# Exclusive-or search end, context steps in VectorE's two waits, and ten more gathered steps ahead of the build

## The reference

```python
q = (xb @ w_query).reshape(t, PEER_HEADS, 2, HALF_KEY)
s = jnp.einsum('thik,hink->thin', q, sub_keys)
v_half, i_half = lax.top_k(s, TOPK)                      # best 16 of 128, for each half
cand = v_half[:, :, 0, :, None] + v_half[:, :, 1, None, :]
cand_idx = i_half[:, :, 0, :, None] * N_KEYS + i_half[:, :, 1, None, :]
top_v, top_pos = lax.top_k(cand, TOPK)                   # best 16 of the 256 sums
idx = take_along_axis(cand_idx, top_pos)                 # expert numbers
g = softmax(top_v)
act = gelu(einsum('thkd,td->thk', expert_u[idx], xb))
out = einsum('thk,thkd->td', g * act, expert_v[idx])
```

## Time and profile before

| what | value |
|---|---|
| median of 3 runs | 2578.82 us (2571.86 to 2583.09) |
| the profiled execution: its own time | 2583.05 us |
| its span, first to last instruction | 2581.2 us |
| TensorE busy | 2300.2 us (89%) |
| VectorE busy | 1797.7 us (70%) |
| POOL busy / ScalarE busy | 1179.9 us (46%) / 635.8 us (25%) |
| DMA: moved, mean | 705.28 MB, 273 GB/s |

### The profile page before, as it was taken

One profiled execution on the slowest core, in us unless ns is written; L12 is line 12 of the kernel. 1 busy time (PEld: TensorE's weight loads), 2 busy tenths in 40 slices (PEclk: granted clock), 3 DMA queues, 4 the chain that ended last, 5 costly groups with the idle time before them and its releaser, 6 DMA issues.

```text
span 2581.2 us, 26507 instructions
## 1 busy us (share of the span) xinstructions
PE 2300.2 (89%) x8779; PEld 1451.1 (56%) x8779; DVE 1797.7 (70%) x3184; ACT 635.8 (25%) x1564; POOL 1179.9 (46%) x979
## 2 busy tenths in 40 slices
PE   6988888898899997999989999978799999999960
PEld 1545454454566443487668887856566666644420
DVE  2657676645600789778778898899676767657678
ACT  2325435231211113411322112199111111110010
POOL 0022231221000346667542235477557786876865
PEclk8999999999999998999999999999899999999985
DMA  8211101107585678999874578999999999999997
GB/s 308 74 33 58 41 24 41 49 33 296 164 284 178 213 298 324 370 369 413 320 268 160 223 280 322 351 365 412 417 379 419 378 411 409 383 400 372 414 389 288
DMA packets 235577, 705.28 MB, mean 273 GB/s; under 512 B 22910, under 2 KB 47614, under 8 KB 234052
## 3 DMA queue, kind: packets, MB, share of 16 engines
q0 software_dynamic: 117936, 429.44, 43.1%
q1 hardware_dynamic: 116948, 272.27, 28.4%
q10 hardware_dynamic: 576, 2.10, 0.2%
HBM read 690.23 MB, written 13.50 MB: 273 GB/s over the span
## 4 chain that ended last, share of the span: by engine, by line
PE 31%; DVE 22%; POOL 17%; DMA 15%; issue 11%; ACT 3%; SPq 1%; DVEq 0%; ACTq 0%; POOLq 0%
PE bank L960 13%; POOL arena L1785 7%; POOL arena L1777 7%; DMA arena<-in_peer_v,arena 6%; DMA arena<-in_peer_u,arena 6%; PE bank L809 4%; PE bank L854 2%; DVE arena L2205 2%; DVE arena L2183 2%; DVE arena L1966 2%; PE bank L1112 2%; POOL arena L1834 2%; DVE arena L2129 2%; DVE arena L2126 2%; DVE arena L2128 1%
## 5 line engine op out<-in xcount | busy, mean ns | idle before, releaser
L1777 POOL DMA_INDIRECT arena<-in_peer_u,arena x384 | 489.1, 1274 | 577.7 <-DVE arena L2183 326.5
L2205 DVE SCALAR_TENSOR_TENSOR arena<-arena 128x1024 f32<-128x1024 f32 x381 | 495.3, 1300 | 139.0 <-DMA arena<-in_peer_v,arena 134.3
L2183 DVE CUSTOM_DVE_ANT_0 arena<-arena 128x1024 f32<-128x1024 f32 x384 | 476.4, 1247 | 150.2 <-DMA arena<-in_peer_u,arena 149.6
L1785 POOL DMA_INDIRECT arena<-in_peer_v,arena x384 | 463.9, 1208 | 244.0 <-DVE arena L2205 136.8
L960 PE MATMUL bank<-arena 128*128 128x512 f32 (+1 forms) x1472 | 507.2, 507 | 15.3 <-DMA arena<-in_w_in 5.2
L1220 PE MATMUL bank<-arena 128*128 128x512 f32 x1024 | 452.3, 594 | 13.4 <-DVE arena L2381 9.3
L1182 PE MATMUL bank<-arena 128*128 128x256 f32 x2048 | 455.3, 380 | 7.1 <-ACT arena L1634 6.4
L1182 PEld LDWEIGHTS bank<-arena 128*128 128x128 f32 x2048 | 390.6, 191 | 88.4 <-issue 37.4
L960 PEld LDWEIGHTS bank<-arena 128*128 128x128 f32 x1472 | 282.4, 193 | 236.0 <-issue 201.1
L1220 PEld LDWEIGHTS bank<-arena 128*128 128x128 f32 x1024 | 195.0, 191 | 232.7 <-issue 214.4
L1634 ACT ACTIVATE arena<-bank 128x256 f32<-128x256 f32 x128 | 49.0, 383 | 589.4 <-PE bank L1182 589.4
(11 more groups left out here) (260 smaller groups left out, 2476.6 us busy)
## 6 DMA issues: line engine op xcount, KB each, us to landing
arena<-in_peer_ut SPq DMA_DIRECT2D x128, 512.0 KB, 6.5
arena<-in_peer_v SPq DMA_DIRECT2D x128, 512.0 KB, 6.6
arena<-in_w_in SPq DMA_DIRECT2D x22, 2048.0 KB, 8.1
arena<-in_w_ada_t POOLq DMA_DIRECT2D x32, 512.0 KB, 4.0
arena<-in_w_ssd_out SPq DMA_DIRECT2D x8, 2048.0 KB, 13.2
arena<-in_w_query SPq DMA_DIRECT2D x8, 2048.0 KB, 7.9
arena<-in_w_ada SPq DMA_DIRECT2D x4, 2048.0 KB, 16.3
arena<-in_w_fourier SPq DMA_DIRECT2D x4, 2048.0 KB, 7.7
```

What stands on the lines that cost most here:

```text
L1777: nc.gpsimd.indirect_dma_start(rowbuf[slot], None, a["peer_u"], bass.IndirectOffsetOnAxis(ap=entries(IDX, k), axis=0)).then_inc(row_in[slo ...
L1785: nc.gpsimd.indirect_dma_start(rowbuf[slot], None, a["peer_v"], bass.IndirectOffsetOnAxis(ap=entries(IDX, k), axis=0)).then_inc(row_in[slo ...
L2183: V.tensor_tensor_reduce(out=rowbuf[slot], in0=rowbuf[slot], in1=h2c if item < PH else h2a[:, item // PH - 1, :], scale=1.0, scalar=0.0, o ...
L2205: STT(pv, rowbuf[slot], w, pv, ALU.mult, ALU.add).then_inc(s("vc_used"), 1)
```

## The change

It has three parts. The index lookup of `top` is written in 16-bit integers: each index gets 128 x its place added, the found place is multiplied by 128 too and written twice side by side, the two are combined by an exclusive-or, and the minimum over the sixteen is the index. The table `WITH` gets an entry `POS` of five context steps, which VectorE takes ahead of its wait for x and `pos1`, with a place for gates on ScalarE ahead of the row copies; 12 context steps stand ahead of the search and 11 in it. The gathered steps of tiles 1 and 2 are spread over heads 2 to 7 (32 as before), and `APART_EARLY` goes from 24 to 34, so that 66 and not 56 stand ahead of the build.

```diff
+        "GB1": (3, 3, 3, 3), "SO2": (2, 2, 2, 2), "SO3": (2, 2, 2, 2), "POS": (5, 0, 0, 0),
...
-CTX_BESIDE = (5, 5, 5, 5, 0, 0, 0, 0)
-APART_BESIDE = (0, 0, 0, 0, 8, 8, 8, 8)
-APART_TOP_BESIDE = {2: (0, 1), 6: (2, 3)}
-APART_EARLY = 24
+AHEAD_OF_SEARCH = 12
+CTX_BESIDE = (5, 5, 1, 0, 0, 0, 0, 0)
+APART_BESIDE = (0, 0, 4, 4, 6, 6, 6, 6)
+APART_TOP_BESIDE = {1: (0, 1), 5: (2, 3)}
+APART_EARLY = 34
...
-NORM_TOPS = PH + min(pair[0] for j, pair in APART_TOP_AT.items() if j > NORM_STEP)
+NORM_TOPS = PH + min((pair[0] for j, pair in APART_TOP_AT.items() if j > NORM_STEP), default=2 * PH)
...
             take_so("l", "SO3")                                  # ScalarE
+            between("l", "POS", 0)
             take_rows(8, (0, 1, 2, 3), 1)
...
+            between("l", "POS", 1)
             for n, t in enumerate(WO_ORDER):
...
-            row16 = shp[:, 6, 0:TOPK].unsqueeze(1).broadcast_to([P, 2, TOPK])
-            CP(places[:, 2:4, :], row16)
-            TS(places[:, 0:2, :], row16, float(TOPK), None, ALU.mult)
+            TS(key_place, shp[:, 6, 0:TOPK], float(NKEY), None, ALU.mult)
+            V.memset(shifts[:, 0:1], float(NKEY // TOPK))
+            V.memset(shifts[:, 1:2], float(NKEY))
...
-                CP(i16fs[:, 0:2 * n * TOPK], i16s[:, 0:2 * n * TOPK])
+                TT(flat(i16fs), flat(i16s), key_place.unsqueeze(1).broadcast_to([P, 2 * n, TOPK]), ALU.add)
...
-                ch(TT(e4, place.unsqueeze(2).broadcast_to([P, 2 * n, TOPK, TOPK]),
-                      flat(tijs).unsqueeze(3).broadcast_to([P, 2 * n, TOPK, TOPK]), ALU.is_equal))
-                ch(TT(e4, e4, flat(i16fs).unsqueeze(2).broadcast_to([P, 2 * n, TOPK, TOPK]), ALU.mult))
+                twice = tij16s[:, 0:4 * n * TOPK].rearrange("p (h q c) -> p h q c", h=2, c=2)
+                ch(TT(twice, tijs[:, 0:2 * n * TOPK].rearrange("p (h q) -> p h q", h=2).unsqueeze(3).broadcast_to([P, 2, n * TOPK, 2]),
+                      shifts.unsqueeze(2).unsqueeze(3).broadcast_to([P, 2, n * TOPK, 2]), ALU.mult))
+                e4 = cands[:, 0:256 * n].bitcast(U16).rearrange("p (g k m) -> p g k m", g=2 * n, m=TOPK)
+                by_two = [P, 2 * n, TOPK, TOPK // 2, 2]
+                ch(TT(e4.rearrange("p g k (m c) -> p g k m c", c=2),
+                      flat(i16fs).rearrange("p g (m c) -> p g m c", c=2).unsqueeze(2).broadcast_to(by_two),
+                      tij16s[:, 0:4 * n * TOPK].rearrange("p (g k c) -> p g k c", g=2 * n, c=2).unsqueeze(3).broadcast_to(by_two),
+                      ALU.bitwise_xor))
...
-                    ch(V.tensor_reduce(flat(picks), e4, AX.X, ALU.add))
+                    ch(V.tensor_reduce(flat(picks), e4, AX.X, ALU.min))
...
             merge("l", "SO3")                                    # VectorE
+            beside("l", "POS", 0)
             dve.wait_ge(s("x1_in"), 16)
...
-            context_steps(8)
+            context_steps(AHEAD_OF_SEARCH)
```

More of the change, by code:

```diff
@@ L15 @@
 U32 = mybir.dt.uint32
+U16 = mybir.dt.uint16
 I32 = mybir.dt.int32
@@ L130 @@
         "Z2": (2, 2, 2, 2), "Z3": (2, 2, 2, 2), "GB0": (3, 3, 3, 3), "SO0": (2, 2, 2, 2), "SO1": (2, 2, 2, 2),
-        "GB1": (3, 3, 3, 3), "SO2": (2, 2, 2, 2), "SO3": (2, 2, 2, 2), "WO0": (1, 1, 1, 1), "WO1": (1, 1, 1, 1)}
[2 rows of a table added]
 TOPS_AT = {2: (2, 3), 14: (4, 5), 26: (6, 7)}
@@ L356, in layer_kernel @@
         stat = sb("stat", [P, 64])
-        places = sb("places", [P, 4, TOPK], U32)
+        places = sb("places", [P, 2, TOPK], U32)
+        key_place, shifts = places[:, 0, :], places[:, 1, 0:2].bitcast(F32)
         masks = sb("masks", [P, 2, TOPK], U32)
@@ L472, in layer_kernel @@
         ij_w = [at(kb, 2 * PICKS).rearrange("p (t n) -> p t n", t=2) for kb in (139.25, 140.25)]
-        ij_all = at(139.25, 4 * PICKS).rearrange("p (g n) -> p g n", g=4)
+        ij_all = at(139.25, 2 * PICKS).bitcast(BF16).rearrange("p (g n) -> p g n", g=4)
         d_w = at(109, 2 * PICKS).rearrange("p (t n) -> p t n", t=2)
@@ L499, in layer_kernel @@
         four = at(122, 4 * 64).rearrange("p (i n) -> p i n", i=4)
-        v16s, i16s, tijs, picks = four[:, 0], four[:, 1].bitcast(U32), four[:, 2].bitcast(U32), four[:, 3]
+        v16s, i16s, tijs, picks = four[:, 0], four[:, 1].bitcast(U32), four[:, 2].bitcast(U32), four[:, 3].bitcast(BF16)
         small64 = at(124, 64)
         tvs, tps = small64[:, 0:32], small64[:, 32:64].bitcast(U32)
-        i16fs = small[:, 2].bitcast(BF16)
+        i16fs = small[:, 2].bitcast(U16)
+        tij16s = small[:, 3:5].rearrange("p a b -> p (a b)").bitcast(U16)
         dots = [small[:, 7, 0:TOPK], small[:, 11, 0:TOPK]]
@@ L2164, in top @@
                       ALU.bitwise_and))
-                e4 = cands[:, 0:256 * n].bitcast(BF16).rearrange("p (g k m) -> p g k m", g=2 * n, m=TOPK)
-                place = places[:, 0:4:3 - n, :]
-                ch(TT(e4, place.unsqueeze(2).broadcast_to([P, 2 * n, TOPK, TOPK]),
-                      flat(tijs).unsqueeze(3).broadcast_to([P, 2 * n, TOPK, TOPK]), ALU.is_equal))
-                ch(TT(e4, e4, flat(i16fs).unsqueeze(2).broadcast_to([P, 2 * n, TOPK, TOPK]), ALU.mult))
+                twice = tij16s[:, 0:4 * n * TOPK].rearrange("p (h q c) -> p h q c", h=2, c=2)
[7 more added lines that the diff above has]
+                      ALU.bitwise_xor))
                 if t in WHOLE:
-                    V.tensor_reduce(ij_all[:, :, TOPK * h:TOPK * h + TOPK], e4, AX.X, ALU.add).then_inc(s("topw_done"), n)
+                    V.tensor_reduce(ij_all[:, :, TOPK * h:TOPK * h + TOPK], e4, AX.X, ALU.min).then_inc(s("topw_done"), n)
                 else:
-                    ch(V.tensor_reduce(flat(picks), e4, AX.X, ALU.add))
+                    ch(V.tensor_reduce(flat(picks), e4, AX.X, ALU.min))
                     half = picks[:, 0:n * TOPK], picks[:, n * TOPK:2 * n * TOPK]
```

## The result

The kernel got slower: 2611.42 us (2603.11 to 2616.6, four runs) against 2580.36 (2571.86 to 2583.09) for the kernel before, a ratio of 1.0122 (1.0101 to 1.0144). The forecast was 2582 us and a range of 2561 to 2598, so it lies outside. The medians are 31.1 us apart, so 11 of these are not in the two traces.

A forecast was written before the change was run, and what follows sets the result against it. VectorE's finish of the build and the gathered rows then left set the end. Terms +15.1 + 17.8 - 24.8 - 2.3 - 1.8 + 25.4 - 26.3 = +3.1 us gave 2586.2, or 2582 against the median; own range 2573 to 2592, widened to 2561 to 2598.

The forecast's parts named there:

- The search end: VectorE's double tops: each saves 0.91 us with the exclusive-or at 692 ns; twelve ahead of the build, 10.9 us.
- Rival C: VectorE's tops: the exclusive-or runs at 1.225 us, +6.4 us, 2588 us; counted within the forecast's class, no chance of its own.
- The first wait: ScalarE's gates(6), ahead of the row copies, wait for the 112th u product and move TensorE's chain by 15.1 us.
- The second wait: VectorE ahead of the search waits at `weights(7)` for ScalarE's gates(7) until 1372.2; this adds 17.8 us.
- Rival A: Ahead of the search: the new waits don't bite, as product and gates come early enough; -25 us, 2554 us; chance 0.27.
- The ten steps: Ten more gathered steps on VectorE before the build cost 25.4 us, bounds 25 and 30.
- The rows given back: After the build: twenty fewer gathered rows are left, 10.5 MB at 399 GB/s, saving 26.3 us; bounds 12.8 and 31.
- Rival B: Tail: rows are not given back, only ten v additions leave it; +16.6 us, 2595 us; chance 0.23 with other path lengthening.
- is ahead of VectorE: Before the build: TensorE no longer stands 6.4 us for the search, its blocks end about 8 us later, ahead of VectorE.

The follow-up runs named there:

- e6: The kernel before with 128 unused bytes a partition ahead of the arena, nothing else: 2617.38 us, ratio 1.0066 to the kernel before.
- e9: The kernel before with ten more gathered steps ahead of the build (`APART_EARLY` 34, not 24): 2587.69 us, ratio 0.9952.
- e5: The kernel before with only the new search end, `places` kept at four rows so the arena starts where it did: 2584.06 us, ratio 0.9954.
- e7: The kernel after with `places` of four rows, so the arena is at its old address: 2591.37 us, ratio 0.9985 to the kernel before.
- e8: The kernel after with the arena at its old address and both of ScalarE's gate places moved: 2564.33 us, ratio 0.9863 to the kernel before.
- e11: The kernel after, unchanged, measured again in the third set: 2619.85 us, ratio 1.0076 to the kernel before.
- e12: The kernel before with the arena 64 bytes further: 2619.28 us, ratio 1.0071 to the kernel before.
- e4: The kernel before with only the new search end, `places` shrunk and the arena shifted: 2588.72 us, ratio 1.0047.
- e3: The kernel after with both gate places moved (gates(6) behind the copies, gates(7) earlier), arena still shifted: 2573.36 us, ratio 0.9988 to the kernel before.
- e1: The kernel after with ScalarE's gates(6) behind the sixteen copies, ahead of the first WO0 product: 2592.42 us, ratio 1.0063 to the kernel before.
- e2: The kernel after with ScalarE's gates(7) taken earlier, behind take_h2(3) and ahead of the first scores: 2588.36 us, ratio 1.0047 to the kernel before.
- e10: The kernel after with both gate places moved and the arena back, but without the ten steps (`APART_EARLY` 24): 2590.86 us, ratio 0.9967 to the kernel before.

## Why the prediction was wrong, step by step

On the chip of the second and third set the parts, each measured alone, are: the arena's start +0.66% (e6), the ten steps -0.48% (e9), the search end -0.46% (e5), the two gate waits +1.22% (e7 less e8). They sum to +0.94%; the whole was measured at +0.76% (e11, 0.53 to 0.99). That they add is an assumption: the ten steps are worth 0.48% in the kernel before and 1.04% where the waits are gone.

- **The step that failed** is the first of the parts, "The search end", which was "worked by form": it priced the instructions and left out that the same edit shrinks `places` and so moves the arena, 128 bytes off a multiple of 256. The line stands in the diff of the kernel. Without it the change is at 0.9985 (e7), and the forecast was 2582 / 2578.82 = 1.0012; with it, 1.0076 and 1.0122. The shift alone costs 0.66% (e6; the medians are 21.0 us apart), where the forecast had nothing. It was in no term, no bound and no rival, so the range could not hold it.
- **Where the shift costs**, as far as single profiles show it, is after the build. In the kernel after and in e7 the search takes 204.3 and 203.9 us, and the way from its end to the build 136.9 and 136.9. Ahead of the search the profiles do not agree: against e9, which is the kernel before up to there, e6 starts it 1.3 us earlier and e12 8.7 later, on one chip. From TensorE's last block to the end every shifted kernel takes 11 to 25.5 us more (us; the pairs are in part of two chips):

  | kernel | old start | shifted |
  |---|---|---|
  | before | 90.2 | 105.6 (e6), 101.0 (e12) |
  | search end alone | 83.7 (e5) | 94.8 (e4) |
  | the change | 43.0 (e7) | 65.9 (after), 61.4 (e11) |
  | both gates moved | 41.2 (e8) | 66.7 (e3) |

  The stretch ahead is TensorE's and hardly longer, but the slower packets bring fewer rows in it: when TensorE's last block ends, 363 v additions have begun in e7 and 349 in the kernel after.
- **The search end's own size** was right: the exclusive-or takes 691 ns (forecast 692), the small multiply 292 (290), the add 224 (218 + 20). Rival C is refuted by that. The Trainium skill, "Vector Engine (DVE) Microarchitecture Reference", section 5.1, gives two results a cycle where all streams are of two bytes and the innermost step is one; the trace agrees for an operand that repeats pairs, at 691 ns for 1024 elements. The search was still 3.7 us longer than forecast, and no less so in e7: VectorE waited 6.9 us in it for rows, where the forecast left 2.2 (8.2 less 6.0).
- **The first wait** was forecast at 15.1 us and moved the WO products by 18.6. Of the 3.5 us, 1.4 come from the end of the wait (the copies start at 1257.7, forecast 1256.3), and most of the rest from TensorE's half clock after its idle time (about 2.2, last section).
- **The second wait** was forecast to end at 1372.2 and ended at 1375.8, later by what the first had moved. The mechanism of both is shown by e1, e2, e3 and e8. Rival A, that they don't bite, is refuted.
- **The ten steps** took 30.8 us (1696.7 to 1727.5), a little over the upper bound of 30, and not 25.4: VectorE still waits for the gathered rows there, 5.3 us in nine waits.
- **The rows given back** were sized at 26.3 us. The tail of the kernel after shrank by 24.3, but with the arena back it shrinks much more: from 90.2 us to 43.0 in e7, and from 83.4 (e10) to 41.2 (e8). So this term was too small by some 20 us, and the shift hid it. I had counted twenty rows of bytes. What the traces show is that the last u product comes before TensorE's end (at 2484.7 in e8, 38.1 us before it), so that the rows after it are all v: 365 v additions have begun at TensorE's end in e8 and 341 in e10, whose last u product is at 2515.6, after TensorE's end. The forecast had ten steps cost about what they bring (25.4 against 26.3). They bring 0.5 to 1%. Rival B, that only ten v additions leave the tail, is refuted by e9, with 23 more; in the kernel after, with its slower rows, it was 11 more (349) and no u product left, where before five were.
- **The range, and how near e7 comes.** The forecast's own range, 2573 to 2592, does not come out of the bounds named with it: the extremes of the ten steps, the exclusive-or and the rows given back add up to about 2577 to 2606. No run turns on it. That e7, without the shift, comes so near the forecast (0.9985 against 1.0012) is in part luck too: its build starts at 1727.7 and not near 1715, and its tail is 43.0 us and not 63.
- **TensorE's first half of blocks** is a floor under the build's start. The prediction said that TensorE "is ahead of VectorE" and left it there. In the kernel after this is true by 22.0 us. With the waits gone and no added steps, VectorE is ahead by 21.8 us (e10), and whatever the search saves more is idle time.

Open is why the change costs 1.2% in the result and 0.8% in e11, and why e3's 0.9988 and e8's 0.9863 are 1.3% apart, on different chips, when e6 gives the arena's start 0.66% and e7 against e11 0.91%. An arena at a multiple of 512 bytes was not tried.

## What to carry to other kernels

A table that shrinks moves what is declared behind it: before pricing an edit's instructions, compare where the targets of the transfers start, and keep them where they were (here at a multiple of 256 bytes) if DMA bounds a stretch. When no stretch carries the loss, look for a side effect of the edit, and test it with a kernel that differs in that alone: a table of stretches can hide it where two errors cancel. Steps put ahead of a stage are paid for only if the stage's other input is ready; read the floor (here TensorE's first half of blocks) along with the wait that ends last now.

## What the runs showed of the hardware

**The start of a transfer's target.** Rows of 4096 bytes whose place in a partition starts 64 or 128 bytes off a multiple of 256 take 161 to 162 ns in the median and 169 to 172 at 90%, against 159 and 159, and the kernel before is slower by 0.71% (64 bytes, e12) and 0.66% (128, e6) with no other difference. The mean rises by 2.6% (163.5 to 167.8 ns) for 128 bytes and 2.9% (168.2) for 64; against e9, a kernel with the old start on the same chip (162.7 ns), it is 3.1 and 3.4%. The Trainium skill, "DMA: Bandwidth & Descriptors", section "How a descriptor splits into AXI transactions", says that a descriptor is cut into transactions of 256 bytes that must start at a multiple of 256, and that bytes before an unaligned start still cost beats of 32. The page says it of what a transaction reads, by the vendor's account; here it is the target that starts off the multiple. If it holds for a target too, a row would be 17 transactions instead of 16, and 132 beats instead of 128 at 128 bytes off, 130 at 64; as estimates from that page, 3.1 and 1.6% more beats. The size fits the runs at 128 bytes. At 64 bytes it was not halved, which fits the one transaction more rather than the beats. That this is the mechanism is not shown. I had not counted this rule in the prediction.

**The clock after an idle time.** TensorE in the kernel after, from the end of its last work before the first wait: idle, the row units and transposes, the WO products (columns as above, the third number from the end is the granted clock):

```profile
1241.43:1258.35 16.92, 0.00 (x1) 0.00 (x1) 12.88 (x19) 2.43 (x7) 13.98 (x10) 0.63 1.03 402
1258.35:1266.85 8.50, 7.82 (x48) 7.62 (x48) 8.10 (x10) 4.02 (x7) 6.67 (x7) 0.73 1.02 407
1266.85:1272.90 6.05, 4.29 (x32) 3.40 (x32) 4.61 (x8) 4.34 (x8) 4.20 (x5) 1.00 1.03 408
```

The granted clock fell from 2.4 to 1.2 GHz within the 16.92 us of idle time (a mean of 0.63) and came back within the first 8.5 us of work (a mean of 0.73). The first group of 16 matmuls took 3.78 us, the second 2.40 and the third 2.01. In the kernel before, without the idle time, the clock stood at 1.00 there.
